# Mixture-of-experts stage: half-blocks of 64 rows on two halves of the array, each expert's weights loaded once, plain fp32 copies in a ring of twelve places

## The reference, cut to what matters

```python
group_probs = softmax(xf @ w_group + b_group); p_group, g_idx = top_k(group_probs, 1)
e_logits = (xf @ w_expert + b_expert)[group g_idx]          # 8 experts in each of 4 groups
p_exp, e_local = top_k(softmax(e_logits), 2)
gate = p_group * p_exp / sum(p_exp)
flat_e = g_idx * 8 + e_local                                # 2 experts a token, 2048 rows in all
hid = silu(ragged_dot(xs, w1, group_sizes)) * ragged_dot(xs, w3, group_sizes)
ys  = ragged_dot(hid, w2, group_sizes) * gate               # then summed by token
```

## Time and profile before

| what | us |
|---|---|
| median of 3 runs (lowest to highest) | 3296.64 (3294.38 to 3300.21) |
| span of the profiled execution, first to last instruction | 3290.7 |
| median less that span | 5.9 |
| route's last DVE instruction to the experts' first instruction | 2502.54 to 2503.04 |
| experts stage (first instruction to the final stage's first) | 2503.0 to 3244.2: 741.2 |
| final stage to the end | 3244.2 to 3290.7: 46.5 |

### The profile page before, as it was taken

One profiled execution on the slowest core, in us unless ns is written; L12 is line 12 of the kernel. 1 busy time (PEld: TensorE's weight loads), 2 busy tenths in 40 slices (PEclk: granted clock), 3 DMA queues, 4 the chain that ended last, 5 costly groups with the idle time before them and its releaser, 6 DMA issues. The chain is left out here.

```text
span 3290.7 us, 41076 instructions
## 1 busy us (share of the span) xinstructions
PE 3042.1 (92%) x14800; PEld 2248.1 (68%) x14800; DVE 1593.9 (48%) x2030; ACT 1186.7 (36%) x1709; POOL 1168.4 (36%) x597
## 2 busy tenths in 40 slices
PE   8999999989999989999899998999995999999992
PEld 5666666448888878874487557998644777777772
DVE  4444444431111121447545454445337777777774
ACT  3333233111111112321233222333214777777773
POOL 1100010113434334430033224224002777777774
PEclk9999999999999999999899999999997999999996
DMA  2000001211111132257310014000215999999995
GB/s 98 22 25 20 20 26 42 112 46 49 40 51 51 51 114 92 94 198 250 117 51 7 33 47 166 14 14 32 114 62 202 368 370 366 372 370 373 370 363 210
DMA packets 116005, 445.93 MB, mean 136 GB/s; under 512 B 14626, under 2 KB 15586, under 8 KB 111026
## 3 DMA queue, kind: packets, MB, share of 16 engines
q1 hardware_dynamic: 102452, 392.61, 32.4%
q0 software_dynamic: 7984, 28.66, 2.6%
q10 hardware_dynamic: 5456, 23.10, 1.7%
HBM read 400.13 MB, written 44.10 MB: 135 GB/s over the span
## 5 line engine op out<-in xcount | busy, mean ns | idle before, releaser
L3053 DVE TENSOR_TENSOR moe_w_low<-moe_raw_up,moe_w_high 128x1024 fp32r<-128x1024 f32 x288 | 438.5, 1562 | 153.2 <-ACT moe_w_high L2993 153.2
L2916 POOL TENSOR_TENSOR moe_w_low<-moe_raw_down,moe_w_high 128x1024 fp32r<-128x1024 f32 x144 | 419.5, 2944 | 143.3 <-ACT moe_w_high L3003 143.3
L2993 ACT ACTIVATE moe_w_high<-moe_raw_up 128x1024 fp32r<-128x1024 f32 x288 | 305.1, 1062 | 188.1 <-PE ps L2956 111.5
L91 PE MATMUL ps<-x1T_high,w_up_high 128*128 128x512 f32 x704 | 274.7, 390 | 3.5 <-PEq L3276 3.5
L91 PE MATMUL ps<-x1T_low,w_up_high 128*128 128x512 f32 x704 | 274.4, 390 | 0.0
L91 PE MATMUL ps<-x1T_high,w_up_low 128*128 128x512 f32 x704 | 274.3, 390 | 0.0
L2971 PE MATMUL ps<-moe_w_high,moe_x_high 128*128 128x512 f32 x576 | 228.5, 397 | 4.0 <-DVE moe_x_low L3084 4.0
L2973 PE MATMUL ps<-moe_w_high,moe_x_low 128*128 128x512 f32 x576 | 225.5, 391 | 0.0
L2972 PE MATMUL ps<-moe_w_low,moe_x_high 128*128 128x512 f32 x576 | 225.4, 391 | 0.0
L801 POOL TENSOR_TENSOR w_up_high<-w_up,consts 128x1024 fp32r<-128x1024 f32 x44 | 83.6, 1900 | 382.7 <-PE ps L91 285.2
L279 POOL TENSOR_TENSOR qkv_low<-qkv_raw,qkv_high 128x1024 fp32r<-128x1024 f32 x22 | 53.6, 2436 | 437.5 <-ACT qkv_high L578 437.5
(11 more groups left out here) (468 smaller groups left out, 6562.9 us busy)
## 6 DMA issues: line engine op xcount, KB each, us to landing
moe_raw_up<-in_w SPq DMA_DIRECT2D x288, 512.0 KB, 9.3
moe_raw_down<-in_w SPq DMA_DIRECT2D x144, 512.0 KB, 9.9
w_ada<-in_w_ada SPq DMA_DIRECT2D x48, 512.0 KB, 4.9
w_up<-in_ffn_w_up SPq DMA_DIRECT2D x22, 1024.0 KB, 4.8
w_down<-in_ffn_w_down SPq DMA_DIRECT2D x44, 512.0 KB, 3.4
y_rows<-xT ACTq DMA_DIRECT2D x36, 512.0 KB, 8.3
qkv_raw<-in_attn_w SPq DMA_DIRECT2D x22, 512.0 KB, 3.5
y_rows<-zero_rows SPq DMA_DIRECT2D x1, 8192.0 KB, 29.1
```

The source lines that it names most:

```text
L91: ins = pe.matmul(out, stationary, moving, start=start and n == 0, stop=stop and n == last)
L2916: pool.tensor_tensor(w_low[:, down_slot(k)], raw_down[:, k], w_high[:, down_slot(k)].bitcast(F32), ALU.subtract).then_inc(down_low, 1)
L2993: act.activation(w_high[:, up_slot(n)], raw_up[:, n], ACT.Copy).then_inc(up_high, 1)
L3053: dve.tensor_tensor(w_low[:, up_slot(n)], raw_up[:, n], w_high[:, up_slot(n)].bitcast(F32), ALU.subtract).then_inc(up_low, 1)
```

## The change

The stage works in halves of 64 rows in place of blocks of 128, two halves a step.

- `stage_route`: an expert gets ceil(rows/64) halves, at least one, side by side. `m.owner` has one entry a half, `m.last_half` gives every expert's last half, and `m.last_pair` the last step. The tables of slots work over 32 steps. `at_row` and `before_end` lie in the last place of `raw_down`. SP loads expert 0, then gate2, and after the router's matmuls also the up pieces of expert 1.
- Experts stage, SP: expert after expert, 8 up and 4 down pieces, each expert once. There are two raw places for every piece (`UP_RING = DOWN_RING = 2`). Piece n of expert e waits until piece n of the last half of expert e-2 has been copied, and until piece n of expert e-1 has landed.
- ACT and DVE copy each piece for every half, unrounded, into a ring with twelve places, one for each piece: ACT up 1, 3, 5 and down 0, 2, DVE up 0, 2, 4, 6, 7 and down 1, 3. A copy waits until the half before has used that place. POOL splits nothing any more.
- PE: one fp32 matmul where there were three of fp32r. The stationary tile is 128x64 (the 64 rows of one half). Lane low writes PSUM partitions 0 to 63 and lane high 64 to 127: w1 and w3 for the up pieces, columns 0 to 511 and 512 to 1023 for the down pieces.
- The rows of both halves are gathered and transposed together, once a step, into one buffer; slots without a token are skipped by the gather.
- ACT and DVE read the owners of three halves into registers at the top of a step.
- Rows of y are stored by halves, two DMAs of 64x512 each. The rows of y that are zeroed ahead are 2048 as before, written in pieces of 512 columns.

```diff
-BLOCKS = (TOP * T - EXPERTS) // P + EXPERTS
+ROWS = 64
+HALVES = (TOP * T - EXPERTS) // ROWS + EXPERTS
+STEPS = HALVES // 2
+COPIES = DT + DE // P
+UP_RING = 2
+DOWN_RING = 2
...
+            then(dve.tensor_tensor(before_end, end.unsqueeze(1).to_broadcast([P, HALVES, EXPERTS]),
+                                   iota[:, 0:HALVES].unsqueeze(2).to_broadcast([P, HALVES, EXPERTS]), ALU.is_le))
+            then(dve.tensor_reduce(owner[:], before_end, AX_X, ALU.add))
...
-        RING = 6
+        ring = sb("moe_ring", [P, COPIES, D])
+        x = sb("moe_x", [P, D])
+        UP_BY = {"act": (1, 3, 5), "dve": (0, 2, 4, 6, 7)}
+        DOWN_BY = {"act": (0, 2), "dve": (1, 3)}
...
+        def copy_up(eng, copy, by, h, s, expert, pieces):
+            for n in pieces:
+                if n in UP_BY[by]:
+                    eng.wait_ge(up_loaded[n], 16 * expert + 16)
+                    earlier(eng, up_used, 8 * h + n - 7)
+                    copy(ring[:, up_slot(s, n)], raw_up[:, ds(expert % UP_RING, 1), n].rearrange("p a n -> p (a n)")
+                         ).then_inc(up_copied[by], 1)
...
+            def load_up(e):
+                last = last_of(e - UP_RING)
+                for n in range(UPS):
+                    done, value = copied(UP_BY, up_copied, n, last)
+                    sp.wait_ge(done, value)
+                    sp.wait_ge(up_loaded[n], 16 * e)
+                    sp.dma_start(raw_up[:, e % UP_RING, n], d["w13"][e, :, n]).then_inc(up_loaded[n], 16)
...
+            load_down(1)
+            for e in range(2, EXPERTS):
+                load_up(e)
+                load_down(e)
...
+            def multiply_up(h, s):
+                rows = slice(s * ROWS, (s + 1) * ROWS)
+
+                earlier(pe, hid_done, h - 1)
+                for n in range(UPS):
+                    done, value = copied(UP_BY, up_copied, n, h)
+                    pe.wait_ge(done, value)
+                    for lane, to in enumerate((low, high)):
+                        ins = pe.matmul(ps[to, 2 + s, :], xT[:, n, rows], ring[:, up_slot(s, n), lane * DE:(lane + 1) * DE],
+                                        start=n == 0, stop=n == UPS - 1)
+                    ins.then_inc(up_used, 1)
...
+            def multiply_down(h, s, turned_next=True):
+                pe.wait_ge(hid_out, h + 1)
+
+                pe.wait_ge(y_out, h + 1)
                 for k in range(HT):
+                    done, value = copied(DOWN_BY, down_copied, k, h)
+                    pe.wait_ge(done, value)
+                    if k == HT - 1 and turned_next:
+
+                        pe.wait_ge(hid_done, h + 2)
+                    for lane, to in enumerate((low, high)):
+                        ins = pe.matmul(ps[to, 4 + s, :], hidT[:, k, :],
+                                        ring[:, down_slot(s, k), lane * HALF:(lane + 1) * HALF],
+                                        start=k == 0, stop=k == HT - 1)
                     ins.then_inc(down_used, 1)
...
+            def step(i):
+                h = 2 * i
+                turn_x(i)
+                if not isinstance(i, int):
+                    multiply_down(h - 2, 0)
+                    turn_hidden()
+                pe.wait_ge(x_out, i + 1)
+                multiply_up(h, 0)
+                if not isinstance(i, int):
+                    multiply_down(h - 1, 1)
+                else:
+                    pe.wait_ge(hid_done, 1)
+                turn_hidden()
+                multiply_up(h + 1, 1)
```

More of the change, by code:

```diff
@@ L2852, in over_pairs @@
             with eng.Fori(1, last + 1) as i:
-                for s in range(2):
-                    body(i, s, 2)
+                body(i)
             return last
@@ L2939, in _ @@
+            def step(i):
+                if isinstance(i, int):
+                    gather(0, 1)
+                else:
+                    pool.wait_ge(x_turned, i)
+                    gather(i, i + 1)
+            pool.memset(x[:], 0.0).then_inc(cleared, 1)
+            pool.wait_ge(cleared, 1)
+            last = over_pairs(pool, step)
+            pool.wait_ge(gathered, 16 * last + 16)
+            for s in range(2):
+                pool.wait_ge(stored[s], 32 * last + 48)
         @block.tensor
@@ L3042, in _, with copy, turned_x @@
-            last = over_pairs(act, step)
-            turned_hidden(2 * last + 1)
-            for k in range(HT):
-                raise_down(2 * last + 1, k, end=True)
-            store(2 * last, 0)
-            store(2 * last + 1, 1)
+            def copy(out, in_):
+                return act.activation(out, in_, ACT.Copy)
+            def turned_x(i):
+                act.wait_ge(x_turned, i + 1)
+                earlier(act, up_used, 16 * i)
+                act.activation(xT[:], two_banks(ps, 0), ACT.Copy).then_inc(x_out, 1)
@@ new lines, in step @@
+            def step(i):
+                h = 2 * i
+                inner = not isinstance(i, int)
+                before = owner_of(act, h - 1) if inner else None
+                now, after = owner_of(act, h), owner_of(act, h + 1)
+                copy_up(act, copy, "act", h, 0, now, range(HT))
+                if inner:
+                    gate(h - 1, 1)
+                turned_x(i)
+                copy_up(act, copy, "act", h, 0, now, range(HT, UPS))
+                if inner:
+                    turned_hidden(h - 1)
+                    store(h - 2, 0)
+                    copy_down(act, copy, "act", h - 1, 1, before)
+                copy_up(act, copy, "act", h + 1, 1, after, range(HT))
+                gate(h, 0)
+                copy_up(act, copy, "act", h + 1, 1, after, range(HT, UPS))
+                turned_hidden(h)
+                if inner:
+                    store(h - 1, 1)
+                copy_down(act, copy, "act", h, 0, now)
```

451 lines of the change are left out of this document (186 added, 265 removed).

## The result

The changed kernel takes 3199.99 us (median of 4 runs, 3197.79 to 3204.18) against 3297.11 us before (median of 4, one run more than in the table of before). The ratio is 0.9706, with a 95% interval of 0.9692 to 0.972. The forecast was 3226 us with a range of 3192 to 3280: the time lies inside the range, and the gain is 97 us where 71 were forecast.

A forecast was written before the change was run, and what follows sets the result against it. The prediction took DMA to bound the experts stage, with PE close behind. Replacing its 741.2 us by 672 and taking 1 off outside gave 3220.5 us of span, plus 5.9 to the median: 3226 us, range 3192 to 3280.

The forecast's parts named there:

- A pair at 0.86 us: PE, experts stage: two fp32 matmuls on two lanes run at once, as in the router, 0.86 us a pair.
- A half at 11.8: PE's time for one half: 12 pairs 10.3 us, plus transposes and changes of division; bounds 10.9 and 13.4.
- DMA at 370 GB/s: Transfer rate in the experts stage: one expert's load 17.0 us, 18.2 with gather and store of one half.
- Copies hidden: Copies of weights by ACT (9.0 us a half) and DVE (7.4 to 11.1) stay under PE's 11.8.
- The wait ahead of the fourth down piece: PE waits there for silu and product; three pairs, 2.6 us, cover some 1.8, leaving 0.8 us of slack.
- Two raw places: SP's loads wait for copies of expert e-2's last half, so DMA and PE pace the stage in three parts, 672 us.
- Outside the stage: Route stage with smaller tables: 1 us off, bounds -2 to +2; the median stands 5.9 us above the profiled span.
- PE above 11.8 a half: Rival: PE needs more for each half, through register waits and an in-order chain; 13.5 us gives 3270; chance 0.20.
- lanes in turn: Rival: PE's two lanes don't run at once, a half costs 22.1 us; 3635 us in all; chance 0.06.
- the forecast's own stretch: The range of times given to the forecast itself: 3205 to 3250 us, chance 0.64.
- rival 2: Experts stage: bytes alone set the time, stage 600 us, 3154 us in all; chance 0.05.
- The clock did fall in the DMA-paced stretches: Rival: PE's clock falls to 1.2 GHz there, a half costs 22.1 us, not 18.2; 3429 us in all; chance 0.05.

The follow-up runs named there:

- The doubled loads: Changed kernel with four experts' weights loaded twice, 25 MB more: in the crowded group (10, 11, 12, 14) 3212.46 us, late (19, 21, 23, 27) 3273.44 us.
- The one-lane run: Changed kernel with the w3 product of the up pieces on the same lane as the w1 product: 3459.65 us, ratio 1.0495.
- the five edits: Changed kernel plus idle POOL work 3243.23 us, y stored twice 3223.26, at most six transfers in flight 3203.78, extra up pairs 3301.48, or extra DVE and ACT operations 3251.9.

## Why the prediction was right, point by point

**What bounds it.** Right. DMA paced the kernel before, and the changed one has DMA and PE in turn. The doubled loads show it: 68.7 us late, 13.8 in the crowded group.

**A pair at 0.86 us.** Right, 0.865. The router's 32 short instructions, read for their spacing and not their 592 ns, priced the largest term of the change. The one-lane run confirmed it at +260 us where +260 was expected.

**A half at 11.8.** Measured 11.4: the hidden transposes take 0.39 us (0.66 was an upper end). Over the crowded group the shorter half gives 6.1 of the 24.3 us by which the stage was forecast too long (236 against 374.9 - 145.0 = 229.9). The drain rule of the Trainium skill (TensorEngine Tiling (Array Packing), Tiling Modes) would have given 12.0, at the price that the forecast took for it from rows. The trace has less: the 22.86 us of two halves are 24 pairs at 0.857 us (the pace inside a group), 1.02 for the row transposes, twice 0.39 for the hidden ones, and 0.5 us behind the groups of pairs. Where the row transposes follow, an up group takes 7.02 us, and where down pairs in the same division follow, 6.92: 0.10 us for that change of division. The row of attention, with the same 0.10, was the better guide.

**DMA at 370 GB/s.** This term was mis-sized: the mechanism is right, the late rate is 409 GB/s. An expert takes 16.5 us, not 18.2. From the landing of expert 18's up pieces to that of expert 31's it gives 20.7 us (237 forecast, 216.3 measured), and most of the 5 us at expert 8. Some 0.1 us an expert of it is that a late half gathers 34 rows, not the mean 43 used. The end gives 6 us back (28 from that last landing to the next stage forecast, 34.0 measured): most of the 4.00 us that PE waits there, until ACT has copied the last down pieces, and 1.8 us of clock were not in my sum. I had read 370 as the transfers' own limit, since their share was 0.99. The share was right, but part of the packets within it were long.

**Copies hidden.** Right at the measured 0.695 us. The upper bound of 1.22 us was never tried by itself: with POOL at work the mean is 1.28 us, of copies at 0.69 and at 2.38, and the crowded half grows by 1.4 us. Yet DVE's work adds up to 7 x 1.28 + 2 x 0.69 = 10.3 us a half, which fits. A sum of work doesn't tell which copies come late; an order with waits in it needs more room than that.

**The wait ahead of the fourth down piece.** I argued it hidden with 0.8 us to spare. In the crowded stretch it is. In the late one it costs PE 48.4 us of idle time, for a reason that I had not seen (silu behind copies that wait for DMA), and costs the kernel next to nothing: with silu first the time is the same and the stage 3.3 us shorter. The forecast had named idle time of PE there as a sign that would make it wrong, and PE's granted clock at full as one that would bear it out. The first came and the second did not, both in the stretches that DMA paces, where they hardly move the time: as signs they were too strict.

**Two raw places.** The waits of SP were placed rightly, and their size was underestimated where they decide: one place less was expected, before that run, to cost 120 us and cost 163.7.

**Outside the stage.** Router's matmuls to experts stage: 39.8 us against 41.2, near the -1 forecast. The opening was longer than forecast, first up matmul at 12.2 in place of 10: the first gather lands 6.1 us after its issue, behind four down loads, and 4.4 us where SP holds those loads back. The 5.9 us between span and median was no constant: after, the median is 0.7 above the span. Every timed run whose span is on record takes 1.8 to 2.0 us more than it; the rest of the 5.9 is that the profiled execution of before was a quick one. That is 5.2 of the 26 us by which the time was forecast too long, and no part of the kernel; the profiled execution of the changed kernel came 3.3 us later to the router's matmuls, which takes most of it back.

**Rivals.** PE above 11.8 a half, bytes alone, and lanes in turn did not occur. With the chances as given, the measured 3199.99 us lay under the forecast's own stretch, between it and rival 2: the mechanism was right, and its two largest terms, the load of an expert and the half, were both too long. The clock did fall in the DMA-paced stretches: 0.91 late, and at the very end four down pieces took 5.35 us after 4.00 us of idle:

```profile
3132.96 3.60 PE L2977 MATMUL ps<-moe_ring,moe_hidT 128*64 128x512 f32 x16
...
3140.95 5.35 PE L2977 MATMUL ps<-moe_ring,moe_hidT 128*64 128x512 f32 x16 [4.00 <-ACT moe_ring L3010]
```

That last fall costs 1.8 us on the path. The opening has one more, at a granted clock of 0.54 from 2517 to 2521 us, after 10.40 us of idle time ahead of the row transposes:

```profile
2517.13 8.81 PE L2962 MATMUL ps<-moe_ring,moe_xT 128*64 128x512 f32 x32 [1.11 <-ACT moe_xT L3016]
```

It takes 8.81 us where a group at full clock takes 7.09. What the falls between cost wasn't separated; they lie where PE has idle time.

## What to carry to other kernels

When the sizes of the parts are uneven, work out for each stretch of parts which engine paces it, with the depth of the buffers; a byte or a microsecond has a price only in the stretches that its engine paces, and a mere change of order gave 28 us of stage time here. Look for a short, odd instruction in the trace that already has the form that you are about to use throughout: its spacing, not its duration, is the price. A share of 0.99 says that the transfers were always busy, and not that they could not be faster. And a mean over copies can hide two kinds: look at single ones before calling it the price.

## What the runs showed of the hardware that was not expected

- Two fp32 matmuls of 128x512 with stationary tiles of 64 columns, on two lanes, run at once also with a semaphore wait between every pair: 0.865 us a pair, 1.73 on one lane.
- A DVE copy of 128x1024 fp32 within SBUF takes 0.69 us, and mostly 2.38 us beside POOL operations of the same size on another tile. DVE's product and eviction, which read PSUM, take 0.69 us either way.
- 4 KB packets take 162 to 163 ns in a stretch that DMA fills and 170 to 180 in the 15 us behind a pause of the queue, in the traces of the changed kernel and eleven of its twelve variants. In the kernel before they take 173 without such pauses, for a cause that the five edits tried did not find.
- Some eleven 512 KB transfers in flight or six at most make no difference to the rate (409 GB/s both).
